# Modulation sums of a two-block transformer kernel: products on VectorE in two accumulators, four products with ones per 1024 columns on TensorE

## The chip, the cores and the metric

One core of one Trainium2 chip runs the whole program in one launch. The metric is device time in microseconds (us); the time before is the median of three runs.

## The reference, cut to what matters

Two blocks of a network follow each other on 256 tokens of width 1024. The first runs twice (feed-forward, mixers, feed-forward) and needs no modulation. The second also runs twice (feed-forward, mixer, feed-forward, on 256 tokens and for the most part 256 context tokens too), and each layer shifts, scales and gates its activations by vectors that depend on two condition vectors alone:

```
s_c, s_cc = silu(c), silu(c_ctx)                 # each 1024 numbers
ml = s_c  @ w_mod[i] + b_mod[i]                  # w_mod[i]: 1024 x 9216, float32
mc = s_cc @ w_mod[i] + b_mod[i]
xn = rms_norm(h, g) * (1 + m[scale]) + m[shift]  # three pairs of scale and shift
h  = h + w * m[gate] * y                         # and three gates per layer
```

So two vectors are multiplied with 2 x 1024 x 9216 weights, 72 MB in all, and nothing but the results (2 x 2 x 9216 numbers) is kept. Everything is float32.

## The kernel before

Weights of the large products stream through three raw buffers of 1 MB (slabs). SyncE's queue issues each load when the slab three before it has been read. ScalarE rounds each half of a slab (a part, 128x1024) into `whi` (line 1081), VectorE subtracts it from the raw part into `wlo` (line 1508), and TensorE makes three products per tile: high by high, high by low, low by high (`mm3`, lines 530 to 532). Four buffers of each kind (`NSPLIT`) let the splitting run up to three parts ahead of TensorE. Activations are split the same way.

A feed-forward has 11 groups; a group is a gate slab and an up slab. After the gate ScalarE takes the silu (line 1170), after the up VectorE multiplies (`sg`, line 1645), ScalarE rounds (`hh`, line 1181) and VectorE subtracts (`hl`, line 1651). Then 12 down slabs follow, in two halves of output columns. With points counted in slabs, gate and up of group g are points 2g and 2g+1 and the down slabs are points 22 to 33. Feed-forwards with 256 tokens are `("f1", 0)`, `("f2", 0)`, `("f1", 1)`, `("f2", 1)` of the first block and `("g2", 1)`; those with 512 tokens are `("g1", 0)`, `("g2", 0)`, `("g1", 1)`.

The modulation is worked off beside the seven feed-forwards other than `("g2", 1)`. Its 72 loads of 1 MB (512 rows by 512 columns) go to four buffers `mraw` in a part of the arena that those stages leave free. Tables of points (`MOD_POINTS`) say behind which slab TensorE makes the products of a load, `mod(q)`: four matmuls, one for each 128 rows, in four bands of 32 output rows of one bank, moving 512 float32 columns each (line 544):

```python
for j in range(4):
    pm = pe.matmul(ps[32 * j:32 * j + 32, :], scp[:, 4 * half + j, 4 - 2 * m:36 - 2 * m], mraw[q % NMOD][:, j, :],
                   start=m == half == 0, stop=m == BATCH - 1 and half == 1, skip_group_check=True)
```

`scp` holds the two silu vectors with zeros around them. Six loads (a batch of 1536 columns) gather in bank 7, which is kept for this: the other products go round seven banks (`SEVEN`). ScalarE copies the bank to `modrow` (line 1159; `modrow` lies in `vgain`), four matmuls with `sel` turn the rows to columns and add up the four bands (`mod_turn`, line 555), and VectorE adds the bias into `modc` (line 1610). In the four 256-token feed-forwards the last load of all is used at point `END`, behind the last down slab, ScalarE copies within the following `norm`, and the turn comes in the next stage.

All engines run in program order; every hand-over is a semaphore. The order of VectorE's work is written by hand: in `ffn` it first splits ahead (`ahead(until, ...)`), then takes the modulation's point, then waits for the group's products.

Of the kernel before, what the change touches and what calls it, by code (L numbers as in the profile page):

```python
# [8 lines left out]
ALU = mybir.AluOpType  # L9
# [24 lines left out]
SEVEN = tuple(range(7))  # L34
MODS = (7,)
NMOD = 4
GATES_OF = {("g1", 0): 0, ("g1", 1): 1}
BATCH = 3
END = 33


MOD_BATCHES = {("f1", 0): (0,), ("f2", 0): (1, 2), ("f1", 1): (3, 4), ("f2", 1): (5,),
               ("g1", 0): (6, 7), ("g2", 0): (8, 9), ("g1", 1): (10, 11)}
MOD_POINTS = {1: (9, 13, 17, 21, 25, END), 2: (8, 10, 12, 14, 16, 18, 20, 22, 24, 26, 28, END),
              512: (2, 3, 4, 5, 6, 7, 9, 9, 10, 11, 12, 13)}
# [12 lines left out]
           "turned": "turn ty xst bt wst qkt cols", "scores": "sc rap", "probs_turned": "ptp nptp", "neighbour_scores": "nsp",  # L58
# [4 lines left out]
    "dve": {"parameters": "cols_copied angles lgx lg ctx_ready modc sel", "columns_hi": "xhv", "columns_lo": "xT yT", "attended_lo": "yn",  # L63
# [10 lines left out]
class Ledger:  # L74
# [5 lines left out]
    def __init__(self, nc, ctx, known):  # L80
        self.nc, self.ctx, self.known = nc, ctx, known
        self.events, self.count, self.sems = {}, {}, {}
        self.bank_of, self.freed, self.params = {}, {}, 16
        self.held, self.units = {}, {ring: 0 for ring in (ALL, SCORES, TURNED, VALUES, MODS)}
# [64 lines left out]
class Modulation:  # L149
# [3 lines left out]
    def __init__(self, slabs, w):  # L153
        self.halves, self.uses, self.loads, self.turns, self.first, self.last = [], {}, {}, {}, {}, {}
        for name, batches in MOD_BATCHES.items():
            wide = name[0][0] == "g"
            points = MOD_POINTS[512 if wide else len(batches)]
            first = slabs.index[name, "gate", 0]
            self.first[name], n = len(self.halves), 0
            for b in batches:  # L160
                for m in range(BATCH):
                    l, g = divmod(BATCH * b + m, 18)
                    for half in range(2):
                        q, at = len(self.halves), points[n]
                        src = w["w_mod_2"][l][512 * half:512 * half + 512, 512 * g:512 * g + 512]
                        self.halves.append((b, m, half, src.rearrange("(k p) n -> p k n", p=P), name))
                        self.uses.setdefault((name, at), []).append(q)
                        if wide:
                            ahead = 3 if n < NMOD else at - 1
                        else:  # L170
                            ahead = 28 if at == END else max(6, at - (4 if len(batches) == 1 else 2))
                        self.loads.setdefault(first + ahead, []).append(q)
                        n += 1
                self.turns[name, at + 1] = b
            self.last[name] = len(self.halves) - 1
# [79 lines left out]
def build(nc, w, consts, out, known):  # L255
# [3 lines left out]
    with ExitStack() as ctx:  # L259
# [20 lines left out]
        scp = place("scp", [P, KD, 36])  # L280
# [8 lines left out]
        sel = cols[:, 3, 96:102]  # L289
# [23 lines left out]
        mraw = [arena(f"mraw{i}", [P, 4, 512], o * KB) for i, o in enumerate((28, 36, 72, 80))]  # L313
# [73 lines left out]
        mod_landed = [ctx.enter_context(nc.semaphore(f"mod{i}_landed")) for i in range(NMOD)]  # L387
# [67 lines left out]
        def _(sp):  # L455
# [7 lines left out]
            def slab_range(a, b):  # L463
                for s in range(a, b):
# [6 lines left out]
                    for q in mods.loads.get(s, ()):  # L471
                        name = mods.halves[q][4]
                        if q >= NMOD:
                            sp.wait_ge(*e.at("modk", q - NMOD))
                        if name not in (("f1", 0), ("f1", 1), ("g1", 0)) and q < mods.first[name] + NMOD:
                            sp.wait_ge(*e.at("turn", name, KD - 1))
                        sp.dma_start(mraw[q % NMOD][:, :, :], mods.halves[q][3]).then_inc(mod_landed[q % NMOD], 16)
# [33 lines left out]
        def _(pe):  # L511
            e = Signals(L, "pe")

            def new(*key, ring=ALL):

                turn = ALL if ring is SEVEN else ring
                u = turn[L.units[turn] % len(turn)]
                L.units[turn] += 1
                if u not in ring:
                    u = turn[L.units[turn] % len(turn)]  # L520
                    L.units[turn] += 1
# [12 lines left out]
            def mod(q):  # L534

                b, m, half = mods.halves[q][0:3]
                if q == 0:
                    pe.wait_ge(*e.at("scc"))
                if m == half == 0:
                    new("modp", b, ring=MODS)  # L540
                ps = bank[MODS[0]]
                pe.wait_ge(mod_landed[q % NMOD], 16 * (q // NMOD + 1))
                for j in range(4):
                    pm = pe.matmul(ps[32 * j:32 * j + 32, :], scp[:, 4 * half + j, 4 - 2 * m:36 - 2 * m], mraw[q % NMOD][:, j, :],  # L544
                                   start=m == half == 0, stop=m == BATCH - 1 and half == 1, skip_group_check=True)
                pm.then_inc(*e.inc("modk", q, also=[("modp", b)] if m == BATCH - 1 and half == 1 else []))

            def mod_turn(b):

                if b == 0:  # L550
                    pe.wait_ge(*e.at("sel"))
# [1864 lines left out]
```

## Time and profile before

| | |
|---|---|
| Three runs | 3479.01, 3475.18, 3471.02 us; median 3475.18 us |
| The profiled execution | 3477.2 us, of which the profile's span is 3475.4 us |
| Mean granted TensorE clock | 0.979 |
| TensorE busy | 3323.6 us (96%), 17814 matmul records |
| VectorE busy | 1644.4 us (47%), 2400 instructions |
| ScalarE busy | 1285.0 us (37%), 1765 instructions |
| HBM read | 493.09 MB, 142 GB/s over the span |

Times in the rows below are microseconds from the start of the span unless marked ns. Matmul records of the 128x512 float32 products with `scp` come two to an instruction (576 records for 288 matmuls), those of transposes one to an instruction. The duration of a matmul record is longer than its distance to the next one, because matmuls are pipelined: costs in TensorE's stream are read from starts, not from durations.

### The profile page before, as it was taken

To read this page: it belongs to the slowest core of one execution; us is meant where nothing else is said; L and a number is where in the kernel's file an instruction comes from. 1 tells how busy PE (TensorE), PEld (TensorE's weight loads), DVE (VectorE), ACT (ScalarE), POOL (GpSimd) and SP (SyncE) were. 2 spreads that over 40 slices of the span, in tenths; PEclk is the share of its full clock that TensorE was granted. 3 is DMA by queue.
4 is the path that set the end of the run, shared out by engine and by line. 5 is a ranking of instruction groups with operands and counts; after the bars stand their busy time and mean duration, and the time that the engine had idled before them with its cause. 6 is when DMAs were issued, how large, how long until landed. Compare 5 with 4: busy or idle time off the path is not lost.

```text
span 3475.4 us, 43622 instructions
## 1 busy us (share of the span) xinstructions
PE 3323.6 (96%) x17814; PEld 2749.3 (79%) x17814; DVE 1644.4 (47%) x2400; ACT 1285.0 (37%) x1765; POOL 93.3 (3%) x128
## 2 busy tenths in 40 slices
PE   7999979999999799999999999999999999999898
PEld 7987769889787689777887777777787778877797
DVE  5546755455457655532324444452324333243655
ACT  4445434444445344422223232232223222233543
POOL 0000000000000000000000000000000000021000
PEclk9999979999999899999999999999999999999999
DMA  7654426757554256643333222244233433253254
GB/s 237 210 175 141 142 78 230 249 189 259 189 160 147 84 180 211 215 146 121 104 103 104 73 73 73 73 155 160 87 114 124 159 123 103 92 131 84 84 186 154
DMA packets 354896, 497.00 MB, mean 143 GB/s; under 512 B 12658, under 2 KB 223500, under 8 KB 354700
## 3 DMA queue, kind: packets, MB, share of 16 engines
q1 hardware_dynamic: 351052, 483.69, 42.0%
q0 software_dynamic: 3648, 10.54, 1.5%
q8 instruction: 143, 2.34, 0.3%
q14 instruction: 53, 0.43, 0.0%
HBM read 493.09 MB, written 1.10 MB: 142 GB/s over the span
## 4 chain that ended last, share of the span: by engine, by line
PE 89%; DVE 6%; ACT 2%; issue 2%; DMA 1%; POOL 1%; SPq 0%; DVEq 0%; POOLq 0%; ACTq 0%
PE bank L530 28%; PE bank L532 27%; PE bank L531 27%; PE bank L544 2%; PE bank L943 1%; DVE wlo L1508 1%; PE bank L674 1%; ACT whi L1081 0%; DVE cv L1785 0%; DMA raw<-in_nat_w_qkv_dram 0%; PE bank L689 0%; PE bank L928 0%; DVE bank L2199 0%; POOL small L2267 0%; DVE small L2195 0%
## 5 line engine op out<-in xcount | busy, mean ns | idle before, releaser
L1508 DVE TENSOR_TENSOR wlo<-raw,whi 128x1024 fp32r<-128x1024 f32 (+2 forms) x782 | 944.7, 1215 | 1389.9 <-ACT whi L1081 1388.2
L1081 ACT ACTIVATE whi<-raw 128x1024 fp32r<-128x1024 f32 (+2 forms) x782 | 814.8, 1047 | 1362.7 <-PE bank L532 1322.5
L530 PE MATMUL bank<-xTh,whi 128*128 128x256 f32 (+1 forms) x3200 | 1044.9, 327 | 11.1 <-DVE xTl L1564 5.0
L532 PE MATMUL bank<-xTh,wlo 128*128 128x256 f32 (+1 forms) x3200 | 1036.3, 324 | 0.0
L531 PE MATMUL bank<-xTl,whi 128*128 128x256 f32 (+1 forms) x3200 | 1033.7, 323 | 0.0
L530 PEld LDWEIGHTS bank<-xTh,whi 128*128 128x128 f32 x3200 | 602.6, 188 | 107.9 <-issue 53.3
L531 PEld LDWEIGHTS bank<-xTl,whi 128*128 128x128 f32 x3200 | 602.2, 188 | 51.9 <-issue 0.5
L532 PEld LDWEIGHTS bank<-xTh,wlo 128*128 128x128 f32 x3200 | 602.3, 188 | 51.3
L530 PE MATMUL bank<-whi,hh 128*128 128x512 f32 x968 | 383.5, 396 | 0.0
L531 PE MATMUL bank<-wlo,hh 128*128 128x512 f32 x968 | 382.3, 395 | 0.0
L532 PE MATMUL bank<-whi,hl 128*128 128x512 f32 x968 | 382.3, 395 | 0.0
L530 PE MATMUL bank<-whi,xTh 128*128 128x512 f32 (+3 forms) x800 | 314.1, 393 | 24.7 <-DVE wlo L1508 14.6
L531 PE MATMUL bank<-wlo,xTh 128*128 128x512 f32 (+3 forms) x800 | 312.3, 390 | 0.0
L532 PE MATMUL bank<-whi,xTl 128*128 128x512 f32 (+3 forms) x800 | 311.9, 390 | 0.0
L530 PEld LDWEIGHTS bank<-whi,hh 128*128 128x128 f32 x968 | 181.6, 188 | 53.5 <-issue 8.4
L532 PEld LDWEIGHTS bank<-whi,hl 128*128 128x128 f32 x968 | 181.6, 188 | 44.1
L531 PEld LDWEIGHTS bank<-wlo,hh 128*128 128x128 f32 x968 | 181.6, 188 | 43.7
L530 PEld LDWEIGHTS bank<-whi,xTh 128*128 128x128 f32 x800 | 154.5, 193 | 60.3 <-issue 9.9
L1181 ACT ACTIVATE hh<-sg 128x512 fp32r<-128x512 f32 x121 | 76.5, 633 | 284.3 <-DVE sg L1645 284.3
L532 PEld LDWEIGHTS bank<-whi,xTl 128*128 128x128 f32 x800 | 154.7, 193 | 33.5
L531 PEld LDWEIGHTS bank<-wlo,xTh 128*128 128x128 f32 x800 | 154.7, 193 | 32.5
L1170 ACT ACTIVATE sg<-bank 128x512 f32<-128x512 f32 x121 | 71.5, 593 | 195.6 <-PE bank L532 195.5
(328 smaller groups left out, 2297.4 us busy)
## 6 DMA issues: line engine op xcount, KB each, us to landing
raw<-in_ffn_w_in_dram SPq DMA_DIRECT2D x176, 1024.0 KB, 5.2
raw<-in_ffn_w_out_dram SPq DMA_DIRECT2D x80, 1024.0 KB, 5.1
mraw<-in_w_mod_dram SPq DMA_DIRECT2D x72, 1024.0 KB, 7.4
raw<-in_w_in_dram SPq DMA_DIRECT2D x44, 1024.0 KB, 5.1
raw<-in_ret_w_in_dram SPq DMA_DIRECT2D x24, 1024.0 KB, 5.1
raw<-in_w_branch_dram SPq DMA_DIRECT2D x12, 1024.0 KB, 5.1
raw<-in_nat_w_qkv_dram SPq DMA_DIRECT2D x12, 1024.0 KB, 8.4
raw<-in_ffn_w_out_dram SPq DMA_DIRECT2D x16, 512.0 KB, 3.5
```

Source lines behind the costliest of these rows:

```text
L530: pe.matmul(ps, lh, rh, start=start, stop=False, skip_group_check=True)
L531: pe.matmul(ps, lh, rl, start=False, stop=False, skip_group_check=True)
L532: return pe.matmul(ps, ll, rh, start=False, stop=stop, skip_group_check=True)
L544: pm = pe.matmul(ps[32 * j:32 * j + 32, :], scp[:, 4 * half + j, 4 - 2 * m:36 - 2 * m], mraw[q % NMOD][:, j, :], start=m == half == 0, sto ...
L674: m = pe.transpose(ps[k % 4][:, t * P:(t + 1) * P], xn[:, t, k * P:(k + 1) * P], ident)
L943: m = pe.matmul(ps[:, :], a, rv[:, j, :], start=i == 0, stop=i == len(pairs) - 1)
L1081: nc.scalar.activation(hi, src, ACT.Copy).then_inc(*e.inc("hi", key, part))
L1170: A(sg[:, b, :], unit("gate", name, g, i)[:, :], ACT.Silu).then_inc(*e.inc("sg", name, g, i, frees=("gate", name, g, i)))
L1181: A(hh[:, o:o + 512], sg[:, b, :], ACT.Copy).then_inc(*e.inc("hhi", name, g, i))
L1508: nc.vector.tensor_tensor(lo, src, hi.bitcast(F32), ALU.subtract).then_inc(*e.inc("lo", key, part))
```

## The change

The products with the modulation's weights are made by VectorE. A part is now 1024 columns with all 1024 rows (nine parts per layer, 18 in all), read in four loads of 256 rows by 1024 columns (1 MB each, 72 as before) into two buffers `mraw`. For each 128 rows (a step: 144 of them, 8 to a part) VectorE runs two instructions of 128x1024, one per condition vector: it multiplies the weights by the silu vector, one number per partition, and adds to one of two accumulators `macc` (the first step of a part only multiplies). TensorE then sums over partitions with four products with ones per part (`mod_sums`), and four transposes turn the row to columns. The four sums are in four bands like those of before, 512 float32 columns each. Bank 7 joins the others.

```diff
+PARTS = 9
+MOD_PARTS = {("f1", 0): (0, 1), ("f2", 0): (2, 3, 4), ("f1", 1): (5, 6), ("f2", 1): (7, 8),
+             ("g1", 0): (9, 10, 11), ("g2", 0): (12, 13, 14), ("g1", 1): (15, 16, 17)}
+def mod_point(name, n, i):
+    if name[0][0] == "g":
+        return 1 + i // 2
+    if name == ("f1", 0):
+        return 6 + 5 * i // 4
+    return 4 + 11 * i // 8 if n == 2 else 2 + i
...
+                q = base + i // 2
+                if k % 2 == 0:
...
+                    ahead = point[i - 3] + 4 if i >= 4 else 3
+                    self.loads.setdefault(first + ahead, []).append(q)
+                self.steps.setdefault((name, at), []).append((c, k, q))
+                if k == KD - 1:
+                    late = (1, 2, 3, 4) if name[0][0] == "g" else (2, 3, 5, 6)
+                    for table, n in zip((self.sums, self.rows, self.turns, self.columns), late):
+                        table[name, at + n] = c
...
-                        if q >= NMOD:
-                            sp.wait_ge(*e.at("modk", q - NMOD))
+                        if q >= 2:
+                            sp.wait_ge(*e.at("mod_read", q - 2))
...
+            def mod_sums(name, at):
+                if (name, at) in mods.sums:
+                    c = mods.sums[name, at]
+                    pe.wait_ge(*e.at("mod_step", c, KD - 1))
+                    ps = new("modp", c)
+                    for half in range(2):
+                        for who in range(2):
+                            o = 64 * half + 32 * who
+                            m = pe.matmul(ps[o:o + 32, :], ones[:, 0:32], macc[c % 2][:, who, 512 * half:512 * half + 512],
+                                          start=True, stop=True, skip_group_check=True)
+                    m.then_inc(*e.inc("modp", c))
+                if (name, at) in mods.turns:
+                    c = mods.turns[name, at]
+                    pe.wait_ge(*e.at("modrow", c))
+                    ps = new("modtp", c)
+                    for j in range(4):
+                        m = pe.transpose(ps[:, j * P:(j + 1) * P], modrow[:, j * P:(j + 1) * P], ident)
+                    m.then_inc(*e.inc("modtp", c))
...
+            def mod_steps(name, at):
+                for c, k, q in mods.steps.get((name, at), ()):
+                    dve.wait_ge(mod_landed[q % 2], 16 * (q // 2 + 1))
+                    if c + k == 0:
+                        dve.wait_ge(*e.at("scc"))
+                    if k:
+                        dve.wait_ge(*e.at("mod_step", c, k - 1))
+                    elif c >= 2:
+                        dve.wait_ge(*e.at("modp", c - 2))
+                    for who in range(2):
+                        a, wk, s = macc[c % 2][:, who, :], mraw[q % 2][:, k % 2, :], scc[:, k, who:who + 1]
+                        m = STT(a, wk, s, a, ALU.mult, ALU.add) if k else TS(a, wk, s, None, ALU.mult)
+                    m.then_inc(*e.inc("mod_step", c, k, also=[("mod_read", q)] if k % 2 else []))
```

`END` and the turns in a following stage are gone: the last steps lie at point 24 or 25 of a 256-token feed-forward and at point 12 of a 512-token one, and rows, turns and bias follow within the same stage.

On VectorE, in a group of the 256-token feed-forward `("f2", 0)`, each row a 128-partition instruction, `wlo` the low halves of a weight part, `sg` and `hl` the hidden products, stood before:

```order
L1508 TENSOR_TENSOR wlo_56<-raw_50,whi_52 128x1024
L1508 TENSOR_TENSOR wlo_57<-raw_51,whi_53 128x1024
L1508 TENSOR_TENSOR wlo_58<-raw_51,whi_54 128x1024
L1508 TENSOR_TENSOR wlo_59<-raw_49,whi_55 128x1024
L1645 TENSOR_TENSOR sg<-sg,bank 128x512
L1651 TENSOR_TENSOR hl<-sg,hh 128x512
```

and in the same group now:

```order
L1474 TENSOR_TENSOR wlo_56<-raw_50,whi_52 128x1024
L1474 TENSOR_TENSOR wlo_57<-raw_51,whi_53 128x1024
L1578 SCALAR_TENSOR_TENSOR macc_85<-mraw_84,scc,macc_85 128x1024 x2
L1474 TENSOR_TENSOR wlo_58<-raw_51,whi_54 128x1024
L1474 TENSOR_TENSOR wlo_59<-raw_49,whi_55 128x1024
L1623 TENSOR_TENSOR sg<-sg,bank 128x512
L1631 TENSOR_TENSOR hl<-sg,hh 128x512
L1578 SCALAR_TENSOR_TENSOR macc_85<-mraw_84,scc,macc_85 128x1024 x2
```

Two steps, four instructions of 128x1024, have come into each group: one between the two pairs of weight parts, one behind the hidden products.

On TensorE, in the same feed-forward between the products of a 256-column slab, one of the eleven stretches with a load's four products stood so before:

```order
L530 MATMUL bank<-xTh_74,whi_54 128x256
L531 MATMUL bank<-xTl_75,whi_54 128x256
L532 MATMUL bank<-xTh_74,wlo_58 128x256
L544 MATMUL bank<-mraw_86,scp 32x512 x4
L530 MATMUL bank<-xTh_74,whi_55 128x256
```

and the sums of its first part stand so now, between the halves of a slab's columns as before (the turn, four transposes, stands alike, three points later):

```order
L524 MATMUL bank<-xTh_74,whi_52 128x256
L525 MATMUL bank<-xTl_75,whi_52 128x256
L526 MATMUL bank<-xTh_74,wlo_56 128x256
L537 MATMUL bank<-macc_85,cst 32x512 x4
L524 MATMUL bank<-xTh_74,whi_53 128x256
```

The instruction form is the same (32 output rows, 512 columns, four bands); what has moved is how often it comes: 72 stretches before, 18 now, and 18 turns for 12.

## Rows read from the trace of the kernel before

**Rows 1.** The page: busy time by engine, and the chain that ended last, by engine.

```profile
PE 3323.6 (96%) x17814; PEld 2749.3 (79%) x17814; DVE 1644.4 (47%) x2400; ACT 1285.0 (37%) x1765; POOL 93.3 (3%) x128
...
PE 89%; DVE 6%; ACT 2%; issue 2%; DMA 1%; POOL 1%; SPq 0%; DVEq 0%; POOLq 0%; ACTq 0%
```

**Rows 2.** Instructions on mraw: ns (min/median/max), first and last start; landing of loads.

```profile
L544 PE MATMUL bank<-mraw,scp x576: 592/593/618, 81.4 to 2846.6; 128*32 128x512 f32 x192
...
DMA to landing us min/median/max: 5.0/7.4/14.7
```

**Rows 3.** Timeline of PE in ("f2", 0): start, us, instruction.

```profile
637.20 0.28 PE L532 MATMUL bank<-xTh,wlo 128*128 128x256 f32 x1
637.41 1.06 PE L544 MATMUL bank<-mraw,scp 128*32 128x512 f32 x8
...
638.63 0.28 PE L531 MATMUL bank<-xTl,whi 128*128 128x256 f32 x1
```

**Rows 4.** Timeline of PE in ("g1", 0), one of three places with two loads together.

```profile
1576.87 1.92 PE L544 MATMUL bank<-mraw,scp 128*32 128x512 f32 x16
```

**Rows 5.** Timeline of PE, last start before and second after one turn (L555).

```profile
1564.64 0.39 PE L532 MATMUL bank<-xTh,wlo 128*128 128x512 f32 x1
...
1566.01 0.40 PE L531 MATMUL bank<-xTl,whi 128*128 128x512 f32 x1
```

**Rows 6.** Timeline of PE around the three transposes of turn_parameters.

```profile
29.98 0.28 PE L532 MATMUL bank<-xTh,wlo 128*128 128x256 f32 x1
30.09 0.40 PE L731 MATMUL bank<-cst,rowt 104*128 104x104 f32 x3
...
30.50 0.28 PE L531 MATMUL bank<-xTl,whi 128*128 128x256 f32 x1
```

**Rows 7.** Timeline of DVE, end of ("f1", 0), then end of mixers(0).

```profile
216.85 0.69 DVE L1661 SCALAR_TENSOR_TENSOR X<-bank,X 128x512 f32<-128x512 f32 x1 [2.58 <-PE bank L532]
...
219.12 0.16 DVE L1539 SCALAR_TENSOR_TENSOR small<-small 128x1 f32<-128x1 f32 x1 [1.18 <-ACT junk_a L1094]
...
530.61 0.69 DVE L2008 TENSOR_TENSOR X<-bank,X 128x512 f32<-128x512 f32 x1 [1.18 <-PE bank L532]
...
532.09 0.16 DVE L1539 SCALAR_TENSOR_TENSOR small<-small 128x1 f32<-128x1 f32 x1 [0.40 <-ACT junk_a L1094]
```

**Rows 8.** Groups of DVE by form: busy us, mean ns of one, idle before.

```profile
L1508 DVE TENSOR_TENSOR wlo<-raw,whi 128x1024 fp32r<-128x1024 f32 x756 | 924.7, 1230 | 1361.6 <-ACT whi L1081 1360.0
...
L1785 DVE SCALAR_TENSOR_TENSOR cv<-xr,cols,cv 128x256 f32<-128x256 f32 x48 | 19.5, 480 | 0.1
...
L1899 DVE SCALAR_TENSOR_TENSOR gv<-gv,small,vgain 128x512 f32<-128x512 f32 x4 | 2.8, 748 | 1.7 <-POOL small L2262 1.7
```

**Rows 9.** Timeline of DVE in ("f1", 0): two parts back to back.

```profile
91.45 2.36 DVE L1508 TENSOR_TENSOR wlo<-raw,whi 128x1024 fp32r<-128x1024 f32 x2
```

**Rows 10.** Timeline of DVE in ("f2", 0): hidden products, first part behind them.

```profile
631.93 0.69 DVE L1645 TENSOR_TENSOR sg<-sg,bank 128x512 f32<-128x512 f32 x1 [0.52 <-PE bank L532]
633.39 0.69 DVE L1651 TENSOR_TENSOR hl<-sg,hh 128x512 fp32r<-128x512 f32 x1 [0.77 <-ACT hh L1181]
634.27 1.23 DVE L1508 TENSOR_TENSOR wlo<-raw,whi 128x1024 fp32r<-128x1024 f32 x1 [0.18 <-ACT whi L1081]
```

**Rows 11.** Timeline of ACT in ("f1", 0): one group without modulation.

```profile
53.19 0.60 ACT L1170 ACTIVATE sg<-bank 128x512 f32<-128x512 f32 x1 [1.71 <-PE bank L532]
...
64.50 0.60 ACT L1170 ACTIVATE sg<-bank 128x512 f32<-128x512 f32 x1 [1.70 <-PE bank L532]
```

**Rows 12.** Windows: busy of PE, PEld, DVE, ACT, POOL, then clock, DMA share, GB/s.

```profile
532.00:536.00 4.00, 3.01 (x17) 2.77 (x17) 2.25 (x7) 3.50 (x9) 0.55 (x1) 0.73 0.00 1
...
737.00:741.00 4.00, 1.91 (x18) 1.57 (x15) 1.86 (x4) 3.75 (x8) 0.55 (x1) 1.00 0.01 2
```

**Rows 13.** Timeline of PE: last twelve transposes behind ("f2", 0), then behind mixers(0).

```profile
739.86 1.53 PE L674 MATMUL bank<-cst,xn 128*128 128x128 f32 x12 [1.82 <-DVE xn L1553]
...
533.46 2.53 PE L674 MATMUL bank<-cst,xn 128*128 128x128 f32 x12 [0.99 <-DVE xn L1553]
```

More of the change, by code:

```diff
@@ L153, in __init__ @@
     def __init__(self, slabs, w):
[L154 to L175, printed above, removed]
@@ new lines, in __init__ @@
+        self.halves, self.loads, self.steps, self.sums, self.rows, self.turns, self.columns = [], {}, {}, {}, {}, {}, {}
+        for name, parts in MOD_PARTS.items():
+            first, base = slabs.index[name, "gate", 0], len(self.halves)
+            point = [mod_point(name, len(parts), i) for i in range(KD * len(parts))]
+            for i, at in enumerate(point):
+                c, k = parts[i // KD], i % KD
+                q = base + i // 2
+                if k % 2 == 0:
+                    l, part = divmod(c, PARTS)
+                    src = w["w_mod_2"][l][P * k:P * k + 2 * P, D * part:D * part + D]
+                    self.halves.append((name, q - base, src.rearrange("(k p) n -> p k n", p=P)))
+                    ahead = point[i - 3] + 4 if i >= 4 else 3
[5 more added lines that the diff above has]
+                        table[name, at + n] = c
@@ L312, in build @@
         sg = arena("sg", [P, 2, 512], 88 * KB)
-        mraw = [arena(f"mraw{i}", [P, 4, 512], o * KB) for i, o in enumerate((28, 36, 72, 80))]
+        mraw = [arena(f"mraw{i}", [P, 2, D], (28 + 8 * i) * KB) for i in range(2)]
+        macc = [arena(f"macc{i}", [P, 2, D], (72 + 8 * i) * KB) for i in range(2)]
         modrow = vgain
@@ L386, in build @@
         bank = [ctx.enter_context(nc.psum_tensor(f"bank{i}", [P, 512], F32)) for i in range(BANKS)]
[L387 removed]
+        mod_landed = [ctx.enter_context(nc.semaphore(f"mod{i}_landed")) for i in range(2)]
         landed = [ctx.enter_context(nc.semaphore(f"raw{i}_landed")) for i in range(NRAW)]
@@ L514, in new @@
             def new(*key, ring=ALL):
[L516 to L521, printed above, removed]
+                u = ring[L.units[ring] % len(ring)]
+                L.units[ring] += 1
                 L.bank_of[key] = u
@@ L532, in mm3 @@
                 return pe.matmul(ps, ll, rh, start=False, stop=stop, skip_group_check=True)
[L534 to L546, printed above, removed]
@@ L718, in ffn @@
                 for n in range(2):
-                    ps = {t: new("down", name, n, t, ring=ring) for t in tiles_of(T)}
+                    ps = {t: new("down", name, n, t) for t in tiles_of(T)}
                     k0 = 0
@@ L1106, in norm @@
                         squares(name, t, 1)
-                    if t == 0 and name in PREVIOUS:
-                        mod_rows(PREVIOUS[name], END)
                     if t == T // P:
```

130 lines of the change are left out of this document (45 added, 85 removed).

## The prediction

> **What bounds the kernel now.** I read the page first. TensorE is busy 96% of the span and 89% of the chain that ended last is TensorE's, while VectorE is busy 47% and holds 6% of the chain [rows 1]. So whatever lies in TensorE's stream counts almost in full, and whatever VectorE does counts only where TensorE comes to wait for it. Next I read the instructions on `mraw`: 576 records are 72 loads of eight records [rows 2]. Four matmuls of a load run in four bands at once, so neither the 593 ns of a record nor its multiple is their price. The price is read in TensorE's timeline, from the last start before to the second start behind (the first one behind is late as well). Last I read VectorE's timeline and its groups by form, for how long the new work takes and how far ahead of TensorE the splitting runs.
>
> **The change part by part.**
>
> *Removed, products of the loads.* From 637.20 to 638.63 are 1.43 us, where two steps of the stream take 0.23: a load costs 1.20 us [rows 3]. In the 512-token feed-forwards two loads share a stretch three times; the busy piece is then 1.92 us for 1.06, so the pair costs 2.06 [rows 3, 4]. Of 72 loads four lie at `END`, behind the last product of a feed-forward. The other 68 are 62 alone and three pairs: 62 x 1.20 + 3 x 2.06 = 80.6 us, all in the stream.
>
> *Removed at END.* TensorE waits there anyway, but ScalarE copies the row before it squares X, and VectorE's mean follows. From X's last update to that mean are 2.27 us behind `("f1", 0)` and 1.48 us at a stage end without modulation [rows 7]. Four ends, 0.79 us each: 3.2 us.
>
> *Removed, turns.* From 1564.64 to 1566.01 are 1.37 us for two steps of 0.23: a turn costs 0.91 us [rows 5]. Twelve: 10.9 us.
>
> *Added, sums.* Eighteen stretches of the same form (32 output rows, four bands, 512 float32 columns), 1.20 us each: 21.6 us. They wait for VectorE's eighth step, placed one or two points earlier, and ScalarE's copy has a point of its own before the turn; I take no wait.
>
> *Added, turns.* Four transposes of 128x128. Three transposes in the stream cost 0.52 - 0.23 = 0.29 us [rows 6], so four cost about 0.40: 7.2 us. The bounds are a part of that (if they hide behind neighbours) and the old 0.91, 16.4 us in all.
>
> *Added, VectorE's products.* No row shows the operation at 1024 elements. Its form (two tensors in SBUF, a number per partition) takes 480 ns at 256 and 748 ns at 512 elements [rows 8], so 1.05 ns an element and about 1.28 us at 1024; subtraction of two tensors at 1024 takes 1.23 [rows 8]. Back to back two instructions of 1.23 take 2.36 [rows 9], so the distance is 0.09 less than the duration, and a step of two instructions is about 2.4 us of the queue. 144 steps are some 350 us of VectorE, taking it from 47% to about 57%. The first steps of the 18 parts have one tensor only and are cheaper or at worst equal.
>
> *Does TensorE come to wait?* A 256-token group without modulation lasts 11.31 us on TensorE (silu to silu) [rows 11]. VectorE needs in it four parts at 1.14, 1.46 from `sg` to `hl` (it waits for ScalarE there), and 0.6 for `hl` [rows 9, 10]: 6.6 us. The densest stage is `("f2", 0)` with two steps a group: 6.6 + 4.8 = 11.4 us, plus some 0.2 of semaphores. TensorE's own group is there 11.31 plus its share of sums and turns, (1.20 + 0.40) a part over four groups = 0.4: 11.7 us. So VectorE is just level. The lead is what decides. The fourth part of a group is subtracted by 635.50 [rows 10]; its matmuls begin when three parts have run since 631.9, at 631.9 + 3/4 x 11.31 = 640.4. The lead is 4.9 us, and the step that now stands ahead of that part takes 2.4 of it. The 2.5 left carry a drift of a few tenths per group over ten groups, or a single burst such as the logarithm polynomial in group 5 of `("f1", 0)` (3.7 us of small instructions, in a group with one step). I put 2 us for stalls there in all. The other three have 1.5 to 1.6 steps a group (6.6 + 3.9 = 10.5 us). A 512-token group lasts twice as long on TensorE, 22.6 us by that estimate, and has four steps: four parts, hidden products twice and 9.6 us are some 18 us, with a longer lead. Nothing there.
>
> A page of the Trainium skill speaks against this reckoning: "VectorE: DVE Perf Modes", section "The DRAIN you can't avoid", has the next instruction start only once the pipe is empty, whatever the semaphores. Taken so, each instruction costs its whole duration, the group of `("f2", 0)` about 12.2 us, and the sum would be 2 to 3 us higher. The pair in [rows 9] takes 2.36 and not 2.46 us, so I go by the row.
>
> *Moved, transfers.* The same 72 MB in 72 loads, but two buffers for four. SyncE's queue stands at a load until VectorE has read the one two earlier, with the weight slabs behind it. VectorE reaches that step right after the part that frees the next raw buffer, so the wait adds no more than a step, about 2.4 us, to a slab that is wanted over one slab later. Landing takes 7.4 us in the median and 14.7 at most [rows 2], and three points later the step is due: 17 us in `("f2", 0)`, of which about 5 go by before the issue. I cost it at nothing; without that cover each late landing holds VectorE, and the splitting behind it, for up to 3 us.
>
> *The clock.* Behind mixers(0), an end without modulation, the granted clock averages 0.73 in 532 to 536, while behind `("f2", 0)`, where the load at END fills part of the wait, it is 1.00 [rows 12]. The last twelve transposes take 2.53 for 1.53 us [rows 13] and the first products are slow too: at its lower level of 1.2 GHz the clock costs here about 2 us. Three ends (f1,0; f2,0; f1,1) lose their filling. I expect a fall at one or two: 2.5 us. The page "TensorE: Matmul & The Clock Gate" (Trainium skill, section on the HAM clock gate) says the slow clock is the default and activity lifts it; by that rule alone, work taken out of a waiting stretch can cost more than it gave.
>
> Sum: - 80.6 - 3.2 - 10.9 + 21.6 + 7.2 + 2 + 2.5 = - 61.4 us. The profiled execution took 3477.2 us, so 3415.8; it lies 2 us over the median 3475.18, which would give 3413.8. I say 3415 us.
>
> **The rivals.**
>
> *VectorE binds in the 256-token feed-forwards.* If each of the two instructions paid its full 1.28 us and a semaphore's round of 0.2, a step is 3.0 us and the group of `("f2", 0)` 12.6 us against 11.7: 0.9 x 10 groups less the lead of about 2 = 7 us, and 1 to 2 us in each of the three others: + 11 us, 3426 us. For it: the nearly level budget. Against it: parts back to back show no such round [rows 9].
>
> *Transfers late.* If most landings in the four dense stages ran near 14.7 us [rows 2] for want of two buffers, 36 loads held VectorE 3 us each, and with the lead spent TensorE would see perhaps a quarter of it, + 27 us: 3442 us. Against it: as many bytes per group as before.
>
> *The clock falls at all three ends*: 6 us in place of 2.5, 3419 us. This and a cheaper turn or cover (3405 us) lie inside the range.
>
> *Slower.* The two-tensor form with a scalar runs at half rate at 1024 elements when it adds onto its own output, 2.2 us an instruction, 4.5 a step. Then `("f2", 0)` needs 15.6 us a group for 11.7 (+ 36 over ten groups after the lead), `("f1", 0)` 13.8 for 11.5 (+ 20), the other two 13.2 (+ 17 each), and the 512-token ones 26 for 23 (+ 8 each): + 114 us; in place of the 2 us of stalls above that gives 3527 us. The point from which the change loses is a step of about 4.0 us (2.0 an instruction), where these stalls reach the 63 us otherwise won. Against it: `cv` adds onto its own output too, and its 480 ns lie on the line through 748 [rows 8].
>
> That the change doesn't do what it says is not a rival: the 54 fewer stretches on TensorE stand in the order of its instructions.
>
> **How the numbers follow.** Forecast as summed (3404 to 3421 with its bounds): 0.70, the clock at all three ends included. VectorE binding: 0.14. Transfers late: 0.08. Half rate: 0.05. The rest, 0.03, is a small gain or none for reasons not seen. The range holds forecast and VectorE binding whole, and part of the late transfers: 3403 to 3438. A measurement of this kernel tells about 0.2% (7 us) from no change. Faster has all but the half rate and the rest: 0.93; within 0.2%: 0.02; slower: 0.05.
>
> **What would show it.** TensorE busy down by about 60 us; the products with `macc` 144 records, 20 us busy, in 18 places, each costing 1.2 us of the stream; transposes of the row 0.4 us each time. The new instructions on VectorE at 1.28 us, 350 us in all. TensorE waiting for `wlo` in the feed-forwards not over 5 us in total; if it is tens, VectorE binds, and the idle time of VectorE in `("f2", 0)` tells whether by its own work (none) or by landings (idle ahead of the steps, released by a DMA). A granted clock under 1 at the three stage ends would show the filling gone. The forecast is wrong if the gain is under 45 or over 75 us.

## The result, and the profile after

| | before | after |
|---|---|---|
| Median, us | 3474.6 (4 runs) | 3380.66 (4 runs, 3379.41 to 3390.51) |
| Ratio | | 0.9736, interval 0.9722 to 0.975 |
| The profiled execution's span, us | 3475.4 | 3379.2 |
| Mean granted TensorE clock | 0.979 | 0.98 |

The change gains 94 us where 61 were forecast, so the time lies 22 us below the lower end of the range (3403). The direction was right. The prices of the instructions in the sum came out within 0.05 us a piece, and the third that was missing comes mostly from something that the sum does not hold.

The page of the changed kernel, busy time by engine and the chain that ended last, against [rows 1]:

```profile
PE 3228.2 (96%) x17358; PEld 2751.3 (81%) x17358; DVE 1959.9 (58%) x2699; ACT 1287.1 (38%) x1771; POOL 93.2 (3%) x127
...
PE 88%; DVE 6%; issue 2%; ACT 2%; POOL 1%; DMA 1%; SPq 0%; DVEq 0%; POOLq 0%; ACTq 0%
```

TensorE's busy time fell by 95 us; VectorE's share rose to 58% (about 57% forecast) and holds no more of the chain than before. The instructions on `macc`, and the loads' landing from the page (count, KB, median us):

```profile
L1578 DVE SCALAR_TENSOR_TENSOR macc<-mraw,scc,macc x252: 1276/1279/1286, 72.5 to 2745.8; 128x1024 f32<-128x1024 f32 x126
...
L537 PE MATMUL bank<-macc,cst x144: 592/604/617, 122.1 to 2755.2; 128*32 128x512 f32 x144
L1578 DVE TENSOR_SCALAR macc<-mraw,scc x36: 745/749/754, 64.3 to 2712.5; 128x1024 f32<-128x1024 f32 x36
```

```profile
mraw<-in_w_mod_dram SPq DMA_DIRECT2D x72, 1024.0 KB, 4.8
```

The two-tensor form at 1024 elements takes 1.279 us (1.28 forecast from the line through 480 and 748 ns), the first step of a part 0.749. Loads land in 4.8 us in the median, sooner than the 7.4 of before [rows 2].

TensorE's timeline around one sum and around one turn, to be read as in [rows 3, 5]:

```profile
592.69 0.28 PE L526 MATMUL bank<-xTh,wlo 128*128 128x256 f32 x1
592.89 1.07 PE L537 MATMUL bank<-macc,cst 128*32 128x512 f32 x8
...
594.11 0.28 PE L525 MATMUL bank<-xTl,whi 128*128 128x256 f32 x1
...
2777.44 0.39 PE L526 MATMUL bank<-xTh,wlo 128*128 128x512 f32 x1
2777.68 0.60 PE L545 MATMUL bank<-cst,vgain 128*128 128x128 f32 x4
...
2778.34 0.40 PE L525 MATMUL bank<-xTl,whi 128*128 128x512 f32 x1
```

A sum costs 1.42 us less two distances of 0.12, that is 1.18 (1.20 forecast; all 18 lie between 1.18 and 1.20). A turn costs 0.90 less two of 0.227, that is 0.45 (0.40 forecast).

VectorE's timeline in `("f2", 0)`, the densest stage, one whole group from `sg` to `sg`:

```profile
617.73 0.69 DVE L1623 TENSOR_TENSOR sg<-sg,bank 128x512 f32<-128x512 f32 x1 [0.48 <-PE bank L526]
619.19 0.69 DVE L1631 TENSOR_TENSOR hl<-sg,hh 128x512 fp32r<-128x512 f32 x1 [0.77 <-ACT hh L1148]
619.80 2.47 DVE L1578 SCALAR_TENSOR_TENSOR macc<-mraw,scc,macc 128x1024 f32<-128x1024 f32 x2
622.19 0.23 DVE L1588 TENSOR_TENSOR modc<-bank,cols 128x8 f32<-128x8 f32 x2
622.34 2.35 DVE L1474 TENSOR_TENSOR wlo<-raw,whi 128x1024 fp32r<-128x1024 f32 x2
624.61 2.48 DVE L1578 SCALAR_TENSOR_TENSOR macc<-mraw,scc,macc 128x1024 f32<-128x1024 f32 x2
627.00 2.35 DVE L1474 TENSOR_TENSOR wlo<-raw,whi 128x1024 fp32r<-128x1024 f32 x2
629.27 0.68 DVE L1623 TENSOR_TENSOR sg<-sg,bank 128x512 f32<-128x512 f32 x1
```

The group lasts 11.54 us, VectorE stands idle in it only for ScalarE (0.77), and the second `sg` comes without a wait: VectorE is level with TensorE, as the 11.4 against 11.7 us of the forecast said. From a step's start to the part behind it are 2.39 us (619.80 to 622.19, 624.61 to 627.00), so the second instruction of a pair starts 1.19 behind the first, 0.09 before that one's 1.28 are over. The Trainium skill's rule that the forecast weighed ("VectorE: DVE Perf Modes", section "The DRAIN you can't avoid") would have 2.56 for the pair; this row does not show it. The same section lets a next instruction that is not held start earlier, and this row agrees with that exception.

TensorE's waits for `wlo`, before and after (total us, times, longest):

```profile
PE bank L530 <- DVE wlo L1508: 14.6, 4, 3.7
```

```profile
PE bank L524 <- DVE wlo L1474: 16.3, 4, 4.2
```

The four waits of before are still four, and none has come in a feed-forward. All four are in the two stages mixers(0) and mixers(1). The 2 us put down for stalls were not spent.

**Where the surplus is.** TensorE's plain products have another distance from each other (the time from one start to the next), also in stages that have no modulation. In a row `bank<-whi,hh` the first name is the operand that moves, here 512 columns of the weights, and the second is the stationary one. The first and the last start of the 528 products of the down slabs with `hh` in a 512-token feed-forward, one behind the other without a pause, before and after:

```profile
1716.56 0.39 PE L530 MATMUL bank<-whi,hh 128*128 128x512 f32 x1
...
1839.52 0.39 PE L532 MATMUL bank<-whi,hl 128*128 128x512 f32 x1
```

```profile
1665.03 0.39 PE L524 MATMUL bank<-whi,hh 128*128 128x512 f32 x1
...
1784.48 0.40 PE L526 MATMUL bank<-whi,hl 128*128 128x512 f32 x1
```

122.96 us over 527 distances are 0.2333 us, 119.45 are 0.2267. Where 256 columns of the activations move, it goes the other way. In `("g2", 1)`, which has no modulation, a stretch of 1055 distances before and one of 1054 after:

```profile
3280.13 0.36 PE L530 MATMUL bank<-xTh,whi 128*128 128x256 f32 x1 [1.56 <-DVE xTl L1564]
...
3404.47 0.28 PE L532 MATMUL bank<-xTh,wlo 128*128 128x256 f32 x1
```

```profile
3181.63 0.41 PE L525 MATMUL bank<-xTl,whi 128*128 128x256 f32 x1
...
3309.94 0.28 PE L526 MATMUL bank<-xTh,wlo 128*128 128x256 f32 x1
```

0.1179 us went to 0.1217. Summed over all distances under 0.3 us between two plain products, by kind: hidden products as the stationary operand 2878 distances, -18.7 us; transposed activations stationary 2003, -12.8; other stationary operands 635, -3.8; activations moving with 512 columns 3683, -8.4; with 256 columns 5841, +16.3. Together -27.4 us.

No instruction of these was changed. What the change also did stands in two lines of its diff that are not shown above:

```diff
-        scp = place("scp", [P, KD, 36])
+        scc = place("scc", [P, KD, 2])
```

`place` gives out each partition's bytes one buffer behind the other. `scp` had 1152 bytes, `scc` has 64. So all that is placed behind it, the small tables, the transposed activations `xTh`/`xTl` and the arena with `hh` and `hl`, starts 1088 bytes earlier, while `whi` and `wlo`, placed ahead of it, stay. From `whi` to `xTh` there were 61248 bytes (239 times 256, and 64), now 60160 (235 times 256). Below, the **place** of a buffer is this distance modulo 256; the buffers of `whi` and `wlo` lie whole multiples of 4096 bytes from each other, so that it is the same from each.

### The profile page after: what moved, and what is told of

The parts are those of the page before. It is cut to its first block, busy times and chain, and to the rows that moved or that the text cites. A ratio compares the mean times of both kernels' runs of the same rounds, so it can differ in the third digit from the quotient of the medians.

```text
span 3379.2 us, 43166 instructions
## 1 busy us (share of the span) xinstructions
PE 3228.2 (96%) x17358; PEld 2751.3 (81%) x17358; DVE 1959.9 (58%) x2699; ACT 1287.1 (38%) x1771; POOL 93.2 (3%) x127
## 4 chain that ended last, share of the span: by engine, by line
PE 88%; DVE 6%; issue 2%; ACT 2%; POOL 1%; DMA 1%; SPq 0%; DVEq 0%; POOLq 0%; ACTq 0%
PE bank L524 28%; PE bank L525 27%; PE bank L526 27%; DVE wlo L1474 1%; PE bank L913 1%; PE bank L652 1%; PE bank L537 1%; DVE cv L1759 0%; ACT whi L1050 0%; DMA raw<-in_nat_w_qkv_dram 0%; POOL small L2236 0%; PE bank L898 0%; PE bank L667 0%; DVE bank L2173 0%; POOL small L2241 0%
## 5 line engine op out<-in xcount | busy, mean ns | idle before, releaser
L524 PEld LDWEIGHTS bank<-xTh,whi 128*128 128x128 f32 x3200 | 611.3, 191 | 69.1 <-issue 17.6
L526 PEld LDWEIGHTS bank<-xTh,wlo 128*128 128x128 f32 x3200 | 611.1, 191 | 49.2
L525 PEld LDWEIGHTS bank<-xTl,whi 128*128 128x128 f32 x3200 | 611.1, 191 | 48.4 <-issue 0.5
L524 PE MATMUL bank<-whi,xTh 128*128 128x512 f32 (+3 forms) x800 | 310.6, 388 | 26.4 <-DVE wlo L1474 16.3
L1578 DVE SCALAR_TENSOR_TENSOR macc<-mraw,scc,macc 128x1024 f32<-128x1024 f32 x252 | 312.0, 1279 | 3.8
```

The source lines that it names most:

```text
L524: pe.matmul(ps, lh, rh, start=start, stop=False, skip_group_check=True)
L525: pe.matmul(ps, lh, rl, start=False, stop=False, skip_group_check=True)
L526: return pe.matmul(ps, ll, rh, start=False, stop=stop, skip_group_check=True)
L1578: m = STT(a, wk, s, a, ALU.mult, ALU.add) if k else TS(a, wk, s, None, ALU.mult)
```

## The experiments

**The old addresses with the changed kernel.** A buffer of 1088 bytes that nobody uses, behind `scc`:

```diff
         scc = place("scc", [P, KD, 2])
+        place("pad", [P, 272])
```

> The changed kernel with 1088 bytes of padding behind scc, so that every SBUF tensor behind it lies where it lay in the kernel before. Both theories start from this: the changed kernel won 33 us more than the sum, and the starts of plain products are 0.227 us apart in place of 0.233 (down products, 128x512) and 0.120 in place of 0.118 (128x256), also in stages without any modulation. Theory placement: the addresses of the activations' buffers, shifted by 1088 bytes because scp shrank from 1152 to 64 bytes, set that distance. Then this run takes about 3380.7 + 33 = 3413 us, with 0.233 and 0.118 back. Theory rest of the change (bank 7 in the round, fewer stretches in four bands, another instruction stream): 3381 us and 0.227 stay.

Measured: 3405.57 us (3396.09 to 3412.08), ratio 0.9802 (0.9775 to 0.9829). The same stretch as above:

```profile
1668.92 0.39 PE L525 MATMUL bank<-whi,hh 128*128 128x512 f32 x1
...
1791.89 0.40 PE L527 MATMUL bank<-whi,hl 128*128 128x512 f32 x1
```

122.97 us again, 0.2333 each. 25 us of the gain go back with the bytes alone; summed up, the distances say 31 between the two profiled executions. What is left is the kernel that the forecast had costed: a gain of 69 us (59 to 78 by the interval) for 61.

**The new addresses with the kernel before.** `scp` leaves its place for 64 bytes, and lies in a part of the arena that the feed-forwards leave free:

```diff
-        scp = place("scp", [P, KD, 36])
+        place("pad", [P, 16])
+        scp = arena("scp", [P, 32 * KD + 4], 92 * KB)
```

> The kernel before, with scp put behind the arena (rows 32 apart in place of 36) and 64 bytes in its old place, so that every other SBUF tensor lies where it lies in the changed kernel. Theory placement: the starts fall to 0.227 apart (and 0.120 for 256 columns) and the time to 3474.6 - 32 = 3443 us. Theory rest of the change: 3475 us, distances as before.

Measured: 3460.36 us (3455.79 to 3462.94), ratio 0.9963 (0.9952 to 0.9973). Distances are those of the changed kernel in every kind of product (0.2268, 0.2270, 0.2271, 0.1209), and summed up they give -26.8 us. The span fell by 17 us and the medians by 12, where 32 were expected. Most of what is missing lies in mixers(1): it is 5 us longer than before where its distances make it 3 shorter, and its granted clock is lower:

```profile
949.00:1261.00 312.00, 275.41 (x1371) 235.88 (x1371) 196.60 (x360) 140.52 (x217) 11.90 (x12) 0.89 0.40 129
```

```profile
947.00:1256.00 309.00, 272.03 (x1371) 227.94 (x1372) 198.17 (x364) 142.53 (x221) 11.89 (x12) 0.93 0.40 131
```

The first is this run, the second the kernel before: 0.89 for 0.93. All ten executions of this run have a mean granted clock of 0.974 or 0.975 (0.978 to 0.983 in the kernel before, beside them), so here it is not the scatter of one execution. Why this kernel's clock is lower is not known. The move of the bytes speeds up this kernel too, but by half of what the distances say.

**VectorE's products made tiny.** The adding steps run over 16 of 1024 columns; the other 1008 columns of the sums keep their first step alone:

```diff
-                        a, wk, s = macc[c % 2][:, who, :], mraw[q % 2][:, k % 2, :], scc[:, k, who:who + 1]
+                        n = 16 if k else D
+                        a, wk, s = macc[c % 2][:, who, 0:n], mraw[q % 2][:, k % 2, 0:n], scc[:, k, who:who + 1]
```

> The changed kernel with the seven adding steps of every part on 16 of 1024 columns only (the sums are then wrong; loads, waits and TensorE's work stay): 252 instructions of 1.28 us fall to about 0.2. Theory hidden: VectorE's products cost at most 2 us, so 3379 to 3381 us. Rival, that they hold TensorE (stalls for the low halves, or slower reads of SBUF): at least 7 us less, 3374 us or under.

Measured: 3383.76 us (3381.45 to 3390.95). Taking 255 us off VectorE gains nothing: its products are hidden whole. TensorE's distances stay too (0.2268 and 0.1209 in the mean), so these products of VectorE do not set them. The stages with modulation last the same within 0.2 us, except the first, which is 1.4 shorter; there the first dozen products start 0.21 us apart in the changed kernel and 0.12 in this run, ahead of any step on `macc`. The 3 us more are the mixers' stages, one 7 longer and one 2 shorter, of which more below.

**VectorE's products made twice.** The other direction; each adding product goes into the sums twice:

```diff
+                    if k:
+                        link(m)
+                        for who in range(2):
+                            a, wk, s = macc[c % 2][:, who, :], mraw[q % 2][:, k % 2, :], scc[:, k, who:who + 1]
+                            m = STT(a, wk, s, a, ALU.mult, ALU.add)
```

> The changed kernel with every adding step made twice, the second pair behind a wait for the first (sums wrong): 4.9 us a step. By the budget of the prediction VectorE then needs 6.6 + 9.8 = 16.4 us a group in (f2, 0) for TensorE's 11.9, and binds in the other 256-token stages and a little in the 512-token ones: about + 120 us, 3500 us, with TensorE waiting for wlo by tens of us per stage. If the lead or the gaps of VectorE are larger than I reckoned, under + 60 us.

Measured: 3543.21 us (3539.57 to 3546.12), ratio 1.02 (1.0177 to 1.0222), 163 us over the changed kernel for the 120 expected. TensorE's waits, and VectorE in `("f2", 0)`:

```profile
PE bank L524 <- DVE wlo L1474: 87.4, 38, 4.0
...
PE bank L537 <- DVE macc L1583: 34.0, 10, 4.7
```

```profile
668.96 0.68 DVE L1628 TENSOR_TENSOR sg<-sg,bank 128x512 f32<-128x512 f32 x1
...
671.01 2.47 DVE L1578 SCALAR_TENSOR_TENSOR macc<-mraw,scc,macc 128x1024 f32<-128x1024 f32 x2
673.52 2.48 DVE L1583 SCALAR_TENSOR_TENSOR macc<-mraw,scc,macc 128x1024 f32<-128x1024 f32 x2
...
685.51 0.68 DVE L1628 TENSOR_TENSOR sg<-sg,bank 128x512 f32<-128x512 f32 x1
```

A doubled step is 4.91 us, a group 16.55. The forecast's arithmetic for its slower rival gives 6.6 + 2 x 4.9 = 16.4. By it `("f2", 0)` would lose (16.4 - 11.7) x 10 less the lead of some 5, 42 us; it lost 40. The three 512-token feed-forwards lost 18 to 19 each, where the rival had 8. No wait for `wlo` is in them. TensorE stands ahead of the sums, for the last steps on `macc`: 10.6, 12.9 and 10.3 us in the three, here the middle one,

```profile
PE bank L537 <- DVE macc L1583: 12.9, 3, 4.7
```

and their mean granted clock is 0.97 to 0.99 for 1.00. The forecast put the wait of the sums at nothing ("I take no wait"). That holds for the changed kernel, and its slower rival needed a term for it. Of the 163 us such waits make 34, new ones for `wlo` 71 (87.4 less the 16.3 in the mixers); the rest is in shorter waits and in the clock (0.967 for 0.980 over the span). The two runs bound the edge and do not place it: nothing is lost with steps of 2.39 us, 163 us with 4.91. That 2.39 is near the edge is argued from the level group above, not measured.

**Which bytes.** Pads ahead of the transposed activations (`R0`), so that these and the arena move and the small tables stay. The edit of the first:

```diff
+        place("pad", [P, 16])
         R0 = base[0]
```

> The changed kernel with 64 unused bytes a partition ahead of the transposed activations xTh/xTl, so that these and everything behind them (the buffers hh, hl, sg, the maps, the accumulators) start 64 bytes later, at odd multiples of 64 bytes as in the kernel before; the small tables, whi and wlo stay. Theory A (it matters whether the operands of the products start at a multiple of 128 bytes): the distance of neighbouring products with hh as the stationary operand goes from 0.227 back to 0.233 us, that of the 512-column products with xT moving from 0.227 to 0.229, that of the 256-column ones from 0.120 to 0.118, and the time to about 3405 us. Theory B (a coarser position decides, the remaining 1024 bytes of the shift): the distances stay at 0.227 and 0.120 and the time at 3381 us.

> The changed kernel with 128 unused bytes ahead of the transposed activations. If multiples of 128 bytes decide (theory A): nothing changes, 0.227, 0.120 and 3381 us. If multiples of 256 bytes or more do (theory B): the distances change in some class of products.

> The changed kernel with 192 unused bytes ahead of the transposed activations, the fourth of the places 64 bytes apart: these and all behind them start 192 bytes (64 short of a multiple of 256) from the weights' place. If any place but a multiple of 256 costs the 512-column products the same: 0.2333 us with hh stationary, 0.229 to 0.233 with the transposed activations moving, 0.114 to 0.118 for the 256-column ones (as in the run that put these alone there), some 3400 to 3410 us. If this place is a still better one for 512 columns: below 0.227 us, and a time below 3362 us.

> The changed kernel with 512 unused bytes ahead of the transposed activations. If only the place within 256 bytes decides: 0.227 and 0.120 us, 3381 us. If a coarser place does too: another distance in some class of products.

Measured, one execution each, with the mean distances over the longest stretches of one kind without a pause:

| place of activations and arena | run | us | `hh` stationary | 512 columns of activations moving | 256 columns |
|---|---|---|---|---|---|
| 0 | changed kernel | 3380.66 | 0.2267 | 0.2268 | 0.1201 to 0.1217 |
| 0 | 512 bytes ahead | 3372.41 | 0.2267 | 0.2268 | 0.1201 |
| 64 | 64 bytes ahead | 3408.47 | 0.2333 | 0.2289 | 0.1179 to 0.1196 |
| 128 | 128 bytes ahead | 3425.67 | 0.2324 to 0.2333 | 0.2324 to 0.2333 | 0.1188 to 0.1205 |
| 192 | 192 bytes ahead | 3403.59 | 0.2289 | 0.2333 | 0.1134 to 0.1189 |

The 64 bytes give back the times of the old addresses, so it is not the small tables, and not the 1024 bytes of the shift. A multiple of 128 is not enough, so theory A falls too, and 512 change next to nothing: what counts, as far as these pads tell, is the place within 256 bytes. Place 0 is the fastest of the four for 512 columns and the slowest for 256.

**Whose place.** Two more edits move one operand at a time. First the arena alone, by 64 bytes put behind the activations:

```diff
+        place("pad", [P, 16])
         A0 = base[0]
```

> The changed kernel with 64 unused bytes behind the transposed activations: these stay where they are in it, and the buffers behind them (hh and hl among them) start 64 bytes later, at odd multiples of 64 bytes. If each operand's own start decides: the products with hh as the stationary operand at 0.233 us (some 4900 of them, +30 us at 6 ns), those with the transposed activations moving stay at 0.227 and 0.120; about 3405 to 3411 us. If only the transposed activations' start decides: 0.227 for all and 3381 us.

Measured: 3413.52 us. Products with `hh` at 0.2333 (122.97 us for 527 distances), those with the activations at 0.2268 and 0.1209 in the mean, as in the changed kernel. Each product goes by its own operands. Of the 33 us over the changed kernel the distances make 22.6; the two mixers' stages alone are 17 us longer together, of which their distances make 2, and the mixer between `("g1", 1)` and `("g2", 1)` is 5 us shorter.

Then everything, by 64 bytes ahead of the first buffer:

```diff
+        place("pad", [P, 16])
         raw = [place(f"raw{i}", [P, SLAB]) for i in range(NRAW)]
```

> The changed kernel with 64 unused bytes ahead of everything, so that all buffers start 64 bytes later and the distances between them stay. Between the weights whi/wlo and the transposed activations there are 60160 bytes in the changed kernel, 235 times 256; in the kernel before 61248, 239 times 256 and 64. If the position of the two operands to each other decides (both in the same place of 256 bytes): distances of products stay at 0.227 and 0.120 us, time 3381 us. If the place of each in the partition decides by itself: 0.233 and 0.229 as in the run with 64 bytes ahead of the transposed activations, and 3408 us.

Measured: 3392.12 us in one execution, and the distances of the changed kernel in every kind, to the fourth digit:

```profile
1672.86 0.39 PE L525 MATMUL bank<-whi,hh 128*128 128x512 f32 x1
...
1792.31 0.40 PE L527 MATMUL bank<-whi,hl 128*128 128x512 f32 x1
```

So it is the position of the two operands to each other that decides, not where either lies. The 11 us over the changed kernel lie in mixers(1) (+7) and in the mixer between `("g1", 1)` and `("g2", 1)` (+3). The windows of mixers(1), after and in this run (busy of PE, PEld, DVE, ACT, POOL, then clock, DMA share, GB/s):

```profile
913.00:1217.00 304.00, 265.37 (x1366) 225.25 (x1364) 198.01 (x359) 142.05 (x220) 11.88 (x12) 0.93 0.40 133
```

```profile
914.00:1225.00 311.00, 273.98 (x1364) 234.47 (x1364) 198.34 (x359) 141.84 (x220) 11.67 (x12) 0.90 0.39 130
```

The same work, 7 us apart by the granted clock, 0.93 or 0.90. The changed kernel has such an execution of its own: three of its four took 3379 to 3381 us at a mean clock of 0.98, one 3390.51 at 0.975, and this run's is 3392.12 at 0.976. With the run with 512 bytes (8 us under the changed kernel, of which distances make 2) I take this for the scatter of single executions; one execution each does not prove it.

**A place of their own for the 256-column activations.** If each operand decides for its own products, both kinds can have their best place. A first try had 128 bytes ahead of `R0`, and `xTh256`/`xTl256` 64 bytes earlier:

```diff
+        place("pad", [P, 16])
+        place("pad2", [P, 16])
         R0 = base[0]
...
-              256: (place("xTh256", [P, KD, 256], F32R, off=R0), place("xTl256", [P, KD, 256], F32R, off=R0 + 8 * KB))}
+              256: (place("xTh256", [P, KD, 256], F32R, off=R0 - 64), place("xTl256", [P, KD, 256], F32R, off=R0 + 8 * KB - 64))}
```

> The changed kernel with 128 unused bytes ahead of the transposed activations, and with the 256-column ones alone (xTh256, xTl256) 64 bytes earlier, at an odd multiple of 64 bytes. If the start of each operand decides for its own products: 256-column products at 0.118 us, 512-column ones and those with hh at 0.227, and a time of 3381 - 12 = about 3366 us, faster than both kernels. If it doesn't hang on the operand itself: 0.120 us, and 3381 us.

Measured: 3413.93 us. The 256-column distances fell (0.1209 to 0.1175 in the mean, at place 64), but the 128 bytes had put the 512-column operands at place 128 (0.2324 to 0.2333), which the run beside it showed to be bad. With 256 bytes in place of the 128 the 512-column operands are at place 0 again and the 256-column ones at 192:

```diff
+        place("pad", [P, 64])
         R0 = base[0]
```

> The changed kernel with 256 unused bytes ahead of the transposed activations, and the 256-column ones alone 64 bytes earlier: all 512-column operands a multiple of 256 bytes from the weights, the 256-column ones 64 bytes short of one. Each operand decides for its own products: 0.227 us where 512 columns move, 0.1150 to 0.1185 instead of 0.1203 where 256 columns of the activations do; the feed-forward stages f1,0 and f1,1 at 192 and 191 us and f2,0 some 1 shorter, as in the run with 128 bytes, everything else as in the changed kernel: 3381 - 10 = about 3371 us, faster than both kernels. Against it: the 1024 and 512 byte places matter too, then 0.227 is lost and the time is 3410 us.

Measured: 3361.73 us (3355.93 to 3367.9), ratio 0.9676 (0.9652 to 0.9701) to the kernel before: faster than both. `("g2", 1)`, to be held against the two stretches of 1055 and 1054 distances above:

```profile
3171.85 0.41 PE L526 MATMUL bank<-xTl,whi 128*128 128x256 f32 x1
...
3293.30 0.28 PE L527 MATMUL bank<-xTh,wlo 128*128 128x256 f32 x1
```

121.45 us, 0.1152 each, for 0.1217 in the changed kernel. 512-column distances stay (0.2267). By the distances it gains 20.8 us over the changed kernel, by the medians 19; the intervals (3354 to 3371 us by this one's ratio, 3378 to 3388 by the other's) don't meet.

## Why the prediction was wrong in size and right in direction

**The step that failed** is the frame of "The change part by part". It costs what the diff removes, adds and moves on the engines, and takes all other work as unchanged. The diff also moved buffers. The sum has no term for the distances of the plain products, of which over 15,000 lie behind one another in this kernel, and 1% of their time (they take some 2,800 us) is nearly half the gain forecast. No rival covered it, and the bound "wrong if the gain is over 75 us" was drawn from the terms listed.

Term by term, against the profiled spans (3475.4 to 3379.2, 96 us):

- Loads and turns removed, -80.6 and -10.9: 72 and 12 stretches are gone; nothing in the runs speaks against their prices.
- END, -3.2. TensorE in the changed kernel at the end of `("f1", 0)`:

```profile
213.74 0.39 PE L526 MATMUL bank<-whi,hl 128*128 128x512 f32 x1
...
219.08 0.36 PE L524 MATMUL bank<-xTh,whi 128*128 128x256 f32 x1 [0.54 <-DVE xTl L1543]
```

  5.34 us from last to first product. Before, the same wait stood between starts at 216.43 and 222.54, 6.11 us; 0.77 saved for 0.79 forecast.
- Sums, +21.6: 18 x 1.19 = 21.4. Turns, +7.2: 18 x 0.44 = 7.9.
- Stalls, +2: none.
- Clock, +2.5: the fall at one end came (+1.3), and a gain elsewhere outweighed it in this pair of executions. Of the three ends that lost their filling one fell to the lower level:

```profile
213.00:220.00 7.00, 4.21 (x29) 3.25 (x29) 4.52 (x10) 5.11 (x12) 1.81 (x4) 1.00 0.06 7
718.00:721.00 3.00, 2.70 (x13) 2.71 (x14) 2.75 (x6) 3.00 (x8) 0.00 (x0) 0.50 0.03 7
...
910.00:917.00 7.00, 4.20 (x29) 3.25 (x28) 4.43 (x9) 5.01 (x12) 1.47 (x4) 1.00 0.04 6
```

  Behind `("f2", 0)` the granted clock is 0.50 (1.2 GHz), and the twelve transposes there take 2.82 us for 1.53 [rows 13], 1.3 us. Behind the two others it stayed at 1.00. More came from a stretch that the forecast did not look at, mixers(0), where before and after differ like the two mixers' windows above. A row of each, over 54 us of it (the work in the two is not quite the same):

```profile
441.00:495.00 54.00, 38.35 (x166) 33.09 (x166) 25.24 (x71) 19.87 (x54) 2.44 (x1) 0.62 0.13 39
```

```profile
441.00:495.00 54.00, 38.25 (x208) 30.84 (x208) 32.24 (x82) 22.63 (x58) 0.00 (x0) 0.84 0.17 59
```

  The stage went from 313.8 to 304.9 us; some 3 us of that are distances, the other 6 the clock. That the change did this is not shown, and it may be luck of the execution: in the same execution of the kernel before, mixers(1) ran at 0.93, and the changed kernel's work with other pads has both mixers' stages at 0.93 (512 bytes) or at 0.89 (the arena alone).

Measured terms: -80.6 - 3.1 - 10.9 + 21.4 + 7.9 = -65.3, with the distances' -27.4 and the clock's +1.3 - 6 about -97 us, for the 96 seen. The run with the old addresses leaves the distances out and measured -69. So the sum's own terms came within some 8 us; what failed is the term that the sum did not have.

The rivals: VectorE did not bind (no new wait for `wlo`); how thin the lead became no row above measures. Transfers did not come late: two buffers were enough, with landings of 4.8 us. The half rate did not appear (1.279 us). The doubled run gives VectorE about as much to do (4.9 us for seven steps of eight, for the rival's 4.5 in all): the four 256-token stages lost 40, 25, 20 and 21 us for the rival's 36, 20, 17 and 17, and each 512-token one was 10 us over its 8, for the most part by the sums' wait that it had left out.

What stays open: why the position of the two operands to each other matters, and why the 256-column distance takes several values at one place (0.1134 to 0.1189 at place 192 in different stages of one run, and about the same spread at place 64 between two runs). The 512-column distances are not wholly fixed by the place either: at place 64 one long stretch of the run with the old addresses, at the start of `("g1", 0)`, has 0.2333 where its others, and the same stretch of the run with 64 bytes, 1024 bytes away, have 0.2289. The rows show the distances, not what TensorE waits for in them.

## What to carry to other kernels

Read a diff for what it does to addresses: a buffer that shrinks or grows moves all behind it, and the same instructions can then run at another distance. Before costing a change, take the distance of the commonest instructions from first and last start of a long stretch, and ask what would alter it; after it, compare that distance in a stage that the change does not touch. And a pad that restores the old addresses is the cheapest experiment there is: it parts what a change does from where it happens to lie.

## What the runs showed of the hardware that was not expected

- The distance of matmuls with 512 moving columns of this type is 0.2267 us in the best case and 0.2289 to 0.2333 in the others, that with 256 columns 0.1134 to 0.1217 over long stretches, by the place of the stationary and the moving operand to each other within 256 bytes of the partition. Shifting both together changes nothing. The Trainium skill ("TensorE: Matmul & The Clock Gate", section "Back-to-back issue gap") gives for an isolated product at the upper clock 2.5 ns over the columns' time, by which I estimate 216 and 109 ns; the fastest stretches here, 226.7 and 113.4 ns, are 11 and 4 ns above it.
- In "SBUF — State Buffer", section "SBUF: two separate sides", the Trainium skill says that among the engines only the port pair shared by VectorE and GpSimd causes contention, and that TensorE never waits on anyone. The run with the tiny steps agrees: with 255 us less of VectorE's work TensorE's distances stay at 0.2268 and 0.1209. What slows the stream here, by up to 7 ns in 227, is how its own two operands lie.
- The stages mixers(0) and mixers(1) have a mean granted clock of 0.89 to 0.90 or of 0.93, 7 us apart with the same instructions (windows above). Kernels that differ only in unused bytes fell to one side or the other, and the kernel before at the new addresses kept its mean clock of 0.974 to 0.975 in all ten executions.
